# Hybrid attention and MoE block in nine phases: the mix's last tiles in another order, input tiles cleared and constants loaded in an earlier phase

## The reference

```python
mix = from_padded(jnp.concatenate([o_a, o_b], axis=-1)) @ w_o[l]
h = layer_norm(DN_ALPHA * h + mix, ln1_g[l], ln1_b[l])
...
g_idx = jnp.argmax(g_logits, axis=-1)
e_sel = jnp.take_along_axis(e_logits, g_idx[:, None, None], axis=1)[:, 0]
top_v, top_i = lax.top_k(e_sel, TOP_K_IN_GROUP)
gate = jax.nn.softmax(top_v, axis=-1) * g_w
...
xs = xt[row_tok].reshape(nb, MOE_BLOCK, d)
hid = jax.nn.silu(xb @ w_e_gate[e]) * (xb @ w_e_up[e])
y = jnp.zeros_like(xt).at[row_tok].add(ys.reshape(prows, d) * row_g[:, None])
...
h = layer_norm(DN_ALPHA * h + ffn, ln2_g[l], ln2_b[l])
```

## Time and profile before

| what | value |
|---|---|
| median of 3 runs | 2441.41 us (2439.84 to 2442.6) |
| the profiled execution's own time | 2440.79 us |
| its span | 2439.1 us |
| PE busy | 2194.7 us, 90% |
| DVE busy | 1712.5 us, 70% |
| ACT busy | 1489.1 us, 61% |
| POOL busy | 328.3 us, 13% |
| window from / forget from / mix's last tile / route from | 478.0 / 661 / 1465 / 1492.1 us |
| experts from / combine from / end | 1527.6 / 2382.9 / 2439.1 us |

### The profile page before, as it was taken

The page is one execution under the profiler, slowest core; times in us unless marked ns, Lnnn a source line. Parts: engine busy times, 40 slices in busy tenths (PEclk is TensorE's granted clock), DMA queues, the critical chain, the costliest instruction groups (busy, mean ns, idle before and its releaser), DMA issues. The chain is left out here.

```text
span 2439.1 us, 35900 instructions
## 1 busy us (share of the span) xinstructions
PE 2194.7 (90%) x11296; PEld 1787.6 (73%) x11296; DVE 1712.5 (70%) x3164; ACT 1489.1 (61%) x2262; POOL 328.3 (13%) x433
## 2 busy tenths in 40 slices
PE   7999999878789999999989995799999999999980
PEld 6788888655467777777768884688888888788860
DVE  5323231278588888888733346899999999999976
ACT  4323241276577777677633331778888788788867
POOL 0112111100000000000000000222222222222211
PEclk9999999979999999999989996899999999999995
DMA  6536352633341222222033424897887969998838
GB/s 199 179 108 188 111 186 78 172 68 95 104 107 38 68 70 59 70 68 78 18 109 142 150 113 155 293 377 258 272 290 212 300 209 354 325 306 301 271 99 297
DMA packets 220554, 420.62 MB, mean 172 GB/s; under 512 B 47912, under 2 KB 97144, under 8 KB 219288
## 3 DMA queue, kind: packets, MB, share of 16 engines
q1 hardware_dynamic: 187760, 316.08, 38.5%
q0 software_dynamic: 31648, 101.89, 14.5%
q10 hardware_dynamic: 1040, 1.31, 0.2%
HBM read 437.68 MB, written 86.39 MB: 215 GB/s over the span
## 5 line engine op out<-in xcount | busy, mean ns | idle before, releaser
L2476 DVE TENSOR_TENSOR moe_w_lo<-fetch_w_raw,moe_w_hi 128x1024 fp32r<-128x1024 f32 x376 | 435.3, 1218 | 9.7 <-ACT moe_w_hi L2405 9.6
L2405 ACT ACTIVATE moe_w_hi<-fetch_w_raw 128x1024 fp32r<-128x1024 f32 x376 | 368.3, 1052 | 61.2 <-DMA fetch_w_raw<-in_w_e_up_dram 28.6
L2530 PE MATMUL moe_ps_gu<-moe_w_hi,moe_xT_hi 128*128 128x512 f32 x736 | 293.4, 399 | 4.1 <-DVE moe_xT_lo L2487 4.1
L2532 PE MATMUL moe_ps_gu<-moe_w_hi,moe_xT_lo 128*128 128x512 f32 x736 | 289.2, 393 | 0.0
L2531 PE MATMUL moe_ps_gu<-moe_w_lo,moe_xT_hi 128*128 128x512 f32 x736 | 288.6, 392 | 0.0
L1438 ACT ACTIVATE fox_p_hi<-fox_ps_t 128x512 fp32r<-128x512 f32 (+4 forms) x352 | 181.0, 530 | 108.0 <-PE fox_ps_t L1578 107.2
L1505 DVE TENSOR_TENSOR fox_p_lo<-fox_ps_t,fox_p_hi 128x512 fp32r<-128x512 f32 (+4 forms) x352 | 211.0, 611 | 28.8 <-ACT fox_p_hi L1438 27.6
L1578 PE MATMUL fox_ps_t<-ident,fox_s 128*128 128x128 f32 (+1 forms) x1216 | 199.7, 279 | 30.4 <-ACT fox_s L1431 19.5
L2482 DVE TENSOR_TENSOR moe_d_lo<-fetch_d_raw,moe_d_hi 128x1024 fp32r<-128x1024 f32 x184 | 213.0, 1220 | 10.7 <-ACT moe_d_hi L2413 10.7
L1492 DVE CUSTOM_DVE_ANT_0 fox_s<-fox_ps_r,fox_ncum 128x512 f32<-128x512 f32 (+4 forms) x352 | 193.6, 569 | 20.0 <-PE fox_ps_r L1563 12.9
L1431 ACT ACTIVATE fox_s<-fox_s,fox_ntop 128x144 f32<-128x144 f32 (+5 forms) x192 | 173.4, 904 | 47.8 <-DVE fox_ntop L1500 47.2
(11 more groups left out here) (342 smaller groups left out, 4994.2 us busy)
## 6 DMA issues: line engine op xcount, KB each, us to landing
fetch_w_raw<-in_w_e_gate_dram SPq DMA_DIRECT2D x192, 512.0 KB
fetch_w_raw<-in_w_e_up_dram SPq DMA_DIRECT2D x192, 512.0 KB
fetch_d_raw<-in_w_e_down_dram SPq DMA_DIRECT2D x92, 1024.0 KB
ahead_raw<-in_w_in_dram SPq DMA_DIRECT2D x24, 1024.0 KB, 5.3
gates_wide<-in_x_dram SPq DMA_DIRECT2D x16, 512.0 KB
h<-gates_wide POOLq DMA_DIRECT2D x16, 512.0 KB, 3.3
gates_wide<-qT SPq DMA_DIRECT2D x32, 256.0 KB, 4.4
mix_h<-h SPq DMA_DIRECT2D x16, 512.0 KB, 3.6
```

Of the source, the lines that this page charges most:

```text
L2405: nc.scalar.activation(w_hi[:, k], w_raw[:, k].rearrange("p j n -> p (j n)"), ACT.Copy).then_inc(gu_high, 1)
L2476: nc.vector.tensor_tensor(w_lo[:, k], w_raw[:, k].rearrange("p j n -> p (j n)"), w_hi[:, k].bitcast(F32), ALU.subtract).then_inc(gu_split, 1)
L2530: nc.tensor.matmul(out, xT_hi[:, slot, k], w_hi[:, k, cols], start=k == 0, stop=False)
L2532: done = nc.tensor.matmul(out, xT_lo[:, slot, k], w_hi[:, k, cols], start=False, stop=k == KT - 1)
```

## The change

In the window phase the memset of `win_oT` moves on DVE behind `keys_low(0)`, and ACT's wait for it moves to `copy_outputs`. In the mix, `choose_experts` is cut in two calls of `choose_expert`: the first expert is chosen in tile 14 between residual and norm, the second in tile 15 where both were. In tile 15 ACT copies the turned `h1` of tile 14 ahead of the norm, and scales tile 15 ahead of the last `copy_h1T`; POOL's drain before the last store goes. The tiles `x`, `still`, `index0`, `index1`, `gain` and `shift` and two semaphores move into the Space `fetch`, which now also spans `phase_combine`. In the route phase POOL clears `still` and `x` behind its constants, DVE writes the two indexes, and SP loads gain and shift behind the expert's weights.

```diff
             def copy_outputs(n, kv):
+                act.wait_ge(zeroed, 1)
                 act.wait_ge(pv_used, 2 * n + kv + 1)
...
-            act.wait_ge(zeroed, 1)
             queries_high(0)
             keys_high(0)
...
-            nc.vector.memset(oT[:], 0.0).then_inc(zeroed, 1)
...
             queries_low(0)
             keys_low(0)
+            nc.vector.memset(oT[:], 0.0).then_inc(zeroed, 1)
...
-                if is_tile(n, TILES - 2, TILES - 1):
+                if is_tile(n, TILES - 2):
                     nc.gpsimd.drain()
...
+                if is_tile(n, TILES - 1):
+                    copy_h1T(*before(n, slot, use))
                 norm(n, slot, use)
+                if not is_tile(n, 0, TILES - 1):
+                    copy_h1T(*before(n, slot, use))
                 if not is_tile(n, 0):
-                    copy_h1T(*before(n, slot, use))
                     scale_h1(*before(n, slot, use))
                 if is_tile(n, TILES - 1):
+                    scale_h1(n, slot, use)
                     copy_h1T(n, slot, use)
-                    scale_h1(n, slot, use)
...
                 if is_tile(n, TILES - 1):
-                    choose_experts(nc.vector, then, logits, left_x, route, chosen, 0, MIXED_EARLY)
+                    choose_expert(nc.vector, then, logits, left_x, route, chosen, 0, MIXED_EARLY, 1)
                 residual(n, slot, use)
+                if is_tile(n, TILES - 2):
+                    choose_expert(nc.vector, then, logits, left_x, route, chosen, 0, MIXED_EARLY, 0)
                 norm(n, slot, use)
...
                 sp.dma_start(fetch["d_raw"][:, ks], src[:, ks]).then_inc(fetch["dn_in"][half], 16)
+            sp.dma_start(fetch["gain"][:], row_broadcast(t["ln2_g"][0], P)).then_inc(fetch["const_in"], 16)
+            sp.dma_start(fetch["shift"][:], row_broadcast(t["ln2_b"][0], P)).then_inc(fetch["const_in"], 16)
...
             constant(nc.gpsimd.memset(one_x[:], 1.0))
+            constant(nc.gpsimd.memset(fetch["still"][:], 0.0))
+            for i in range(2):
+                constant(nc.gpsimd.memset(fetch["x"][:, i], 0.0))
...
             then(v.tensor_tensor(route["tokens"][:, 0:ROWS], route["tokens"][:, 0:ROWS], codes, ALU.add))
+            for i in range(2):
+                v.tensor_scalar(fetch["index"][i][:], route["tokens"][:, i:i + 1], 0.0, None, ALU.add).then_inc(fetch["indexed"], 1)
...
-            nc.gpsimd.memset(still[:], 0.0).then_inc(cleared, 1)
-            nc.gpsimd.memset(x[:, 0], 0.0).then_inc(cleared, 1)
-            pool.wait_ge(cleared, 2)
             gather(0, 0, 0)
-            nc.gpsimd.memset(x[:, 1], 0.0).then_inc(cleared, 1)
-            pool.wait_ge(cleared, 3)
             gather(1, 1, 0)
...
-            pick_index(0, 0, 0)
-            pick_index(1, 1, 0)
             gu_lows(0, range(0, 4))
...
-                if n == 0:
-                    sp.dma_start(gain[:], row_broadcast(t["ln2_g"][0], P)).then_inc(const_in, 16)
-                    sp.dma_start(shift[:], row_broadcast(t["ln2_b"][0], P)).then_inc(const_in, 16)
...
             phase_experts(nc, ctx, ident, t, route, fetch)
-        phase_combine(nc, ctx, t, route)
+            phase_combine(nc, ctx, t, route, fetch)
```

More of the change, by code:

```diff
@@ L1644, in choose_group, with choose_expert @@
     then(v.tensor_tensor(by_group, by_group, s["hide"][:].unsqueeze(3).to_broadcast([P, K, G, E]), ALU.add))
-def choose_experts(v, then, logits, left_x, route, s, lo, hi):
+def choose_expert(v, then, logits, left_x, route, s, lo, hi, i):
     X, K = N_EXPERTS, hi - lo
     el, cand, first = s["el"], s["cand"], s["first"]
[L1651 to L1662, removed]
+    top = route["top"][i][:, lo:hi]
+    pick = route["first_pick"][:, lo:hi] if i == 0 else s["second"][:]
+    then(v.tensor_reduce(top, el[:], AX.X, ALU.max))
+    then(v.tensor_tensor(cand[:], el[:], top.unsqueeze(2).to_broadcast([P, K, X]), ALU.is_equal))
+    then(v.tensor_tensor(cand[:], cand[:], left_x[:].unsqueeze(1).to_broadcast([P, K, X]), ALU.mult))
+    then(v.tensor_reduce(first[:], cand[:], AX.X, ALU.max))
+    then(v.tensor_tensor(pick, cand[:], first[:].unsqueeze(2).to_broadcast([P, K, X]), ALU.is_equal))
+    if i == 0:
+        then(v.scalar_tensor_tensor(out=el[:], in0=pick, scalar=10 * NEG, in1=el[:], op0=ALU.mult, op1=ALU.add))
+    else:
+        both = logits["x"][:].rearrange("p x t -> p t x")[:, lo:hi]
+        then(v.tensor_tensor(both, route["first_pick"][:, lo:hi], pick, ALU.add))
 def phase_mix(nc, sems, ident, t, logits, route, ahead):
@@ L2129, in _ @@
             choose_group(v, then, logits, left_g, route, chosen, MIXED_EARLY, T)
-            choose_experts(v, then, logits, left_x, route, chosen, MIXED_EARLY, T)
+            for i in range(2):
+                choose_expert(v, then, logits, left_x, route, chosen, MIXED_EARLY, T, i)
             dve.wait_ge(consts, 14)
@@ L2240, in phase_experts @@
         d_lo = m.sb("d_lo", [P, DT, D], F32R)
-        index = [m.sb(f"index{i}", [P, 1], I32) for i in range(2)]
+        index, still, x, indexed = fetch["index"], fetch["still"], fetch["x"], fetch["indexed"]
         code = [m.sb(f"code{i}", [P, 1], I32) for i in range(2)]
@@ L2244, in phase_experts @@
         tick = m.sb("tick", [1, 2])
-        still = m.sb("still", [1, 1])
-        x = m.sb("x", [P, 2, D])
         xT_hi = m.sb("xT_hi", [P, 2, KT, P], F32R)
@@ L2264, in phase_experts @@
         dn_split = m.sem("dn_split")
-        cleared = m.sem("cleared")
         gathering = m.sem("gathering")
         scattering = m.sem("scattering")
-        indexed = m.sem("indexed")
         coded = m.sem("coded")
@@ L2572, in _, with phase_combine @@
             down(2 * pairs - 1)
-def phase_combine(nc, sems, t, route):
+def phase_combine(nc, sems, t, route, fetch):
     with ExitStack() as ctx:
         m = Space(nc, ctx, "out", sems)
-        gain = m.sb("gain", [P, D])
-        shift = m.sb("shift", [P, D])
         eps = m.sb("eps", [P, 1])
@@ L2589, in phase_combine @@
         rstd = m.sb("rstd", [P, 4])
-        const_in = m.sem("const_in")
+        gain, shift, const_in = fetch["gain"], fetch["shift"], fetch["const_in"]
         eps_ready = m.sem("eps_ready")
@@ L2718, in hybrid_block_kernel @@
             fetch = {"w_raw": raw.sb("w_raw", [P, KT, 2, D_EXPERT]), "d_raw": raw.sb("d_raw", [P, DT, D]),
+                     "x": raw.sb("x", [P, 2, D]), "index": [raw.sb(f"index{i}", [P, 1], I32) for i in range(2)],
+                     "still": raw.sb("still", [1, 1]), "gain": raw.sb("gain", [P, D]), "shift": raw.sb("shift", [P, D]),
+                     "indexed": raw.sem("indexed"), "const_in": raw.sem("const_in"),
                      "gu_in": [raw.sem(f"gu_in{i}") for i in range(4)], "dn_in": [raw.sem(f"dn_in{i}") for i in range(2)]}
```

## The result

The changed kernel takes 2447.98 us (median of 12 runs, 2441.11 to 2449.67), the kernel before, on the same chip, 2440.02 (12 runs): ratio 1.0027, 95% interval 1.0017 to 1.0037. It is slower by 0.27%, where 2433.6 was forecast. The profiled execution of the new kernel is the shortest of the 12 (2441.11, span 2439.2), so its stages have to be compared one by one.

The account below looks back on a forecast made before the run. Single-instruction chains set the borders' time, PE's work the experts'. Mix -4.9, route +0.14, experts' start -1.4, combine -2.3 and clears +0.7 sum to -7.8: 2433.0 profiled, 2433.6 as median; range 2430.0 to 2437.3.

Parts of the forecast that it names:

- The step that failed: Experts: PE is busy 98.6%, so the phase keeps its length and only its start can move; change in length 0.
- Mix, -4.9: Last tiles of the mix: an earlier residual and turn for tile 15 let the route phase start 4.9 us earlier.
- rival 2: Tail of the mix: PE keeps its clock in turn and router, 1.2 us more gained, 2432.4; chance 0.09.
- Route, +0.14 and one clear: Route phase: two index instructions add 0.14 us to DVE's chain; one more range clear behind it, at 0.18.
- Rival 3: Route phase: POOL's memsets stop DVE's chain for up to twice 0.97 us, giving 2435.5; chance 0.04.
- Experts' start, -1.4: Start of the experts: marker and gather no longer wait behind a memset, so PE starts 1.4 us earlier.
- Combine, -2.3: Start of the combine phase: without gain and shift loads between, ACT's second tile follows 2.65 behind the first, 2.3 us gained.
- Clears, +0.7: Phase borders: one range clear more behind route, two fewer behind experts, five more at the end; 0.7 us lost.
- Window, 0: Window phase: ACT's first copy starts about 1.0 us earlier, but the wait for win_k_raw absorbs it; gain 0.
- Rival 4: Experts: PE runs out of weights, each wait costing 3.88 us; slower from the fourth on, 2449.1; chance 0.02.
- what would show a step wrong: Signs: route starting at 1486.0 or before, or a longer stretch from the experts' first matmul to their last.

Follow-up runs that it names:

- e5: The kernel before with only x, the indexes, still and 8 KB of room placed ahead of the experts' weights: 2454.85 us (1.0061).
- e9: The change with 96 bytes of room between the experts' split weights and turned inputs (distance 98560): 2433.57 us, 0.9962 to the kernel before.
- e3: The kernel before with only the mix's new order from the change: 2436.50 us (0.9984).
- e4: The kernel before with only the window's moved memset from the change: 2442.76 us (1.0006).
- e15: The kernel before with 64 bytes ahead of the experts' indexes (operand distance 106816): 2453.45 us (1.0057).
- e7: The kernel before with 8 KB of room behind the experts' split weights, moving the turned inputs and all behind them: 2439.20 us (1.0000).
- e2: The kernel before with 32 bytes ahead of the experts' split weights and nothing else changed: 2440.06 us (0.9995).
- e12: The kernel before with 192 bytes of room ahead of the mix's oT_hi (operand distance 79360 instead of 79168): 2436.34 us (0.9980).
- e14: The change with 96 bytes of room ahead of the experts' turned inputs and 128 more ahead of moe_hT_hi: 2436.96 us, 0.9990 to the kernel before.

## Why the prediction was wrong

**The step that failed** is in the first paragraph: PE is busy for 98.6% of the experts, "so that phase is as long as PE's work, and only its start can move". The row says that PE is the bound; it doesn't say that PE's work is fixed. I took the price of a matmul as a constant and costed the move of six tiles into `fetch` at nothing. It raised the price of most of 3312 matmuls (46 blocks of 72), +14.2 in the profile. e5 has the same loss with nothing changed but places (experts 849.7 long), and 96 bytes of room take it back in e9. With it the forecast's sum of -7.8 becomes +6.4; measured are +8.0 by the medians and +6.6 by the ratio.

**The other steps held.** *Mix, -4.9:* -5.1, and e3 alone 4.2. Tile 15's residual came 14.73 behind tile 14's instead of 16.88, the 2.15 forecast; its turn 7.3 behind that, as forecast; the store was issued 9.15 behind it, as forecast; route began 1.6 behind the end of the last logits instead of 1.85, which is the 0.2 by which the gain exceeds the forecast. One row differed: PE's router of tile 14, 1.11 behind the turn, ran at a granted clock of 1.00 and took 1.98; before, after 6.39 of idle time, it ran at 0.50 and took 3.63. It changed nothing, as PE then waited 3.48 for tile 15's `h1`. This was part of rival 2, whose 1.2 did not come: the last turn and router ran at a granted clock of 0.50 and took 1.97 and 3.63.

The text before the prediction counts 13 instructions in the choice, and the forecast 0.60 for each; there are 12, six in each half, and a start every 0.625. It changed nothing: DVE was through with the second half at 1463.0 and waited 1.61 for PE.

*Route, +0.14 and one clear:* +0.6, 0.3 more than forecast. DVE's chain from the phase's start to its end is 34.5 instead of 34.4, as forecast. The 0.3 stand behind the last clear, where POOL's drain at L96 is followed by its next event after 0.40 instead of 0.08 (e9 has 0.40 too); why, no run here shows. Rival 3 is out. POOL cleared both halves of `x` in 1.96 beside DVE's chain, whose 0.26 us instructions still started every 0.29, as in the kernel before. The two views of that stretch, POOL's row and two of DVE's:

```profile
1484.41 1.96 POOL L2114 MEMSET fetch_x<- 128x1024 f32 x2
...
1485.20 0.26 DVE L1655 TENSOR_TENSOR route_c_cand<-route_c_cand,route_left_x 128x96 f32<-128x96 f32 x1
1485.49 0.25 DVE L1656 TENSOR_REDUCE route_c_first<-route_c_cand 128x3 f32<-128x96 f32 x1
```

*Experts' start, -1.4:* PE's first turn came 5.1 behind the phase's start, the first gate/up matmul 9.4 behind instead of 10.8. *Combine, -2.3:* the second tile started 2.66 behind the first. *Clears, +0.7:* from the last `moe_y` to the end 1.8 were won where -2.3, two clears fewer and five more make -1.8.

*Window, 0:* e4 agrees. ACT's wait for `win_k_raw` was 8.55 instead of 6.95 and ended 12.3 behind the phase's start instead of 11.9, so the start gained nothing. That the profiled phase took 176.3 and not 183.3 goes with the granted clock. Windows from 500 to 580 us, before and after (stretch, length, busy us of PE, PEld, DVE, ACT, POOL, PE clock, DMA share, GB/s):

```profile
500.00:540.00 40.00, 32.59 (x161) 21.04 (x160) 31.41 (x109) 30.79 (x60) 2.63 (x3) 0.84 0.26 63
540.00:580.00 40.00, 35.01 (x185) 22.66 (x184) 31.46 (x98) 22.65 (x52) 1.62 (x3) 0.89 0.29 75
```

```profile
500.00:540.00 40.00, 33.11 (x176) 22.58 (x175) 32.61 (x113) 32.71 (x64) 2.63 (x3) 0.91 0.27 68
540.00:580.00 40.00, 34.21 (x195) 22.57 (x196) 35.64 (x115) 25.76 (x60) 2.16 (x4) 1.00 0.36 90
```

It goes from 0.84 and 0.89 to 0.91 and 1.00. The longest phases have the low clock (e15, with the window of the kernel before: 0.84 and 0.89, 183.3 us), those between have one between (e7: 0.88 and 0.95, 179.8). It changes from one execution to the next: in the nine profiles with the moved memset the phase took between 176.3 and 182.3 us, in the eight without it between 179.8 and 183.3. Whether the moved memset shifts these odds by 1 or 2 us stays open.

**The rivals.** Rival 4 had the right side and the right phase, and the wrong mechanism: PE did not run out of weights: its waits in the experts came to 10.8 us, 11.7 before. ACT's waits for `fetch_w_raw` in the experts even fell, from 28.6 to 22.4 us. A longer stretch from the experts' first matmul to their last was named as what would show a step wrong, and did.

e9 is the change with the operands' distance kept at a multiple of 256. It lies 8.1 below the kernel before by the medians and 9.3 by the ratio (6.1 to 12.5), where 7.8 was forecast, so the terms at the borders stand. That its median, of five runs from 2429.54 to 2437.68, is 2433.57 beside the 2433.6 of the forecast is luck.

The range has slips of its own: 1.6 below 2430.7 is 2429.1 and not 2430.0, and its upper end leaves out the 1.0 that the window might lose. With both put right it would still end 10 us below 2447.98.

## What to carry to other kernels

A tile that is moved between allocations moves all tiles behind it (here `moe_w_hi` by 16480 bytes and `moe_xT_hi` by 8192): write down, before and after, the address of each operand of the matmuls that bound a phase, and for matmuls like these, try a distance between moving and stationary operand that is a multiple of 256 bytes (0.68 us per three here, 0.70 at 64, 128 or 160 past one); no run here has another type or width of matmul. Where PE is the bound, measure the pitch of its matmuls and not only its busy share; here up to 0.0067 us per matmul outweighed all gains at four borders together, and 96 bytes of unused SBUF gave it back. When a profile differs from the median of its kernel, compare it stage by stage before believing any total.

## What the hardware showed that was not expected

Streams of matmuls of 512 columns on tiles of type fp32r, at a granted clock of 1.00, start 0.227 us apart (three in 0.68) where moving and stationary operand lie a multiple of 256 bytes apart in a partition, and 0.233 (three in 0.70) at 64, 128 or 160 past one; at 192 past it was 0.229 (0.687). At a multiple of 256 too the first triples behind a turn are slower, 0.78, 0.69 and 0.70 in the kernel before. It holds for weights placed at odd multiples of 32 as well (e2 at 72352, e9 at 88800, both 0.68), in the experts and in the mix (e12, 0.68 for 0.70), with the projection's rows in agreement (0.68), and for each product by itself (e14, 0.68 and 0.70). The rows show no wait inside such a stream, yet its pace goes with the distance between the two addresses: 0.70 at 98464 bytes in the change, 0.68 at 98560 in e9. Why, and why 192 is milder than 64, no run here shows. The rooms also move the tiles behind them, so that a part of other tiles in it is not excluded, though e14's two kinds of products in one block speak against it. No run has 32, 96 or 224 past a multiple.
